# A decoder trunk's odd attention: placement of the sample queries, and the iterations in which sample results are read

## The reference, cut to what matters

```python
# NSA: compressed, selected and window branch, gated;  DSA: an indexer picks the keys
p_c = masked_softmax(s_c, dist_c >= 0);   o_c = p_c @ vc          # compressed keys
p_s = masked_softmax(s_s, mask_s);        o_s = p_s @ sel_v       # selected blocks
p_w = masked_softmax(s_w, mask_w);        o_w = p_w @ kw_v        # window of 256
o_n = gates[..., 0:1] * o_c + gates[..., 1:2] * o_s + gates[..., 2:3] * o_w
isc = relu(qi @ kidx) @ wi;               i_idx = top_k(isc, topk)
o_d = masked_softmax(qd @ kd[i_idx] - m_d * dist) @ vd[i_idx]
return concat([o_n, o_d]) @ w_out
```

## Time and profile before

| | us |
|---|---|
| median of 3 runs | 1462.45 |
| lowest, highest | 1459.09, 1464.04 |
| the profiled execution, its own time | 1457.2 |
| its span in the trace | 1455.3 |
| PE busy | 1395.8 (96%) |
| DVE, ACT, POOL busy | 750.5, 505.5, 398.9 |

### The profile page before, as it was taken

The page is one execution under the profiler, slowest core; times in us unless marked ns, Lnnn a source line. Parts: engine busy times, 40 slices in busy tenths (PEclk is TensorE's granted clock), DMA queues, the critical chain, the costliest instruction groups (busy, mean ns, idle before and its releaser), DMA issues. The chain is left out here.

```text
span 1455.3 us, 27589 instructions
## 1 busy us (share of the span) xinstructions
PE 1395.8 (96%) x11335; PEld 1308.3 (90%) x11335; DVE 750.5 (52%) x1374; ACT 505.5 (35%) x1004; POOL 398.9 (27%) x471
## 2 busy tenths in 40 slices
PE   6999998999999999999899989998999999999996
PEld 5999974899999999999899856776999999999996
DVE  3424777577334343344879755443584343343435
ACT  3321224355213133133532445675454033130311
POOL 3014423464101010016734471022662010010102
PEclk9999999999999999999999989998999999999998
DMA  4343170031313223121522253202223223131301
GB/s 153 118 115 116 30 233 6 3 116 59 117 59 117 72 103 113 62 66 44 118 51 44 59 175 111 59 1 60 87 88 117 68 107 109 66 116 59 117 30 59
DMA packets 87196, 123.86 MB, mean 85 GB/s; under 512 B 24438, under 2 KB 42302, under 8 KB 87040
## 3 DMA queue, kind: packets, MB, share of 16 engines
q1 hardware_dynamic: 82048, 107.00, 23.0%
q0 software_dynamic: 5024, 15.10, 3.5%
HBM read 115.62 MB, written 8.57 MB: 85 GB/s over the span
## 5 line engine op out<-in xcount | busy, mean ns | idle before, releaser
L1025 PE MATMUL ps<-xh,ring_lo 128*128 128x260 f32 (+2 forms) x2496 | 504.3, 283 | 1.4 <-ACT big L1590 1.4
L1025 PEld LDWEIGHTS ps<-xh,ring_lo 128*128 128x128 f32 (+2 forms) x2496 | 383.2, 187 | 3.3 <-ACT big L1590 2.3
L1025 PE MATMUL ps<-xl,wr 128*128 128x260 f32 x1568 | 351.4, 283 | 6.2 <-DVE xl L2060 3.9
L1025 PE MATMUL ps<-xh,wr 128*128 128x260 f32 x1568 | 353.5, 284 | 2.5 <-POOL xl L822 1.2
L1025 PEld LDWEIGHTS ps<-xl,wr 128*128 128x128 f32 x1568 | 255.2, 188 | 8.2 <-DVE xl L2060 5.1
L1025 PEld LDWEIGHTS ps<-xh,wr 128*128 128x128 f32 x1568 | 256.2, 188 | 5.0 <-ACT att L1627 1.4
L840 POOL TENSOR_TENSOR att<-att 128x520 f32<-128x520 f32 (+1 forms) x80 | 77.3, 967 | 548.6 <-DVE att L1986 521.5
L1962 DVE TENSOR_TENSOR ring_lo<-ring,wr 128x1024 fp32r<-128x1024 f32 (+1 forms) x144 | 191.9, 1336 | 62.2 <-ACT wr L1590 62.0
L1025 PE MATMUL ps<-hh,wr 128*128 128x260 f32 x1024 | 222.1, 283 | 0.0
L1025 PE MATMUL ps<-hh,ring_lo 128*128 128x260 f32 x1024 | 221.8, 283 | 0.0
L1025 PE MATMUL ps<-hl,wr 128*128 128x260 f32 x1024 | 221.7, 283 | 0.0
(11 more groups left out here) (353 smaller groups left out, 1679.0 us busy)
## 6 DMA issues: line engine op xcount, KB each, us to landing
ring<-in_w_up SPq DMA_DIRECT2D x16, 2048.0 KB, 7.9
ring<-in_w_down SPq DMA_DIRECT2D x16, 2048.0 KB, 8.0
ring<-in_w_in_e SPq DMA_DIRECT2D x9, 1024.0 KB, 5.4
ring<-in_w_in_e SPq DMA_DIRECT2D x2, 2048.0 KB, 8.5
ring<-in_w_out_e SPq DMA_DIRECT2D x2, 2048.0 KB, 9.1
ring<-in_w_in_o SPq DMA_DIRECT2D x16, 256.0 KB, 5.0
ring<-in_cache_kv POOLq DMA_DIRECT2D x32, 128.0 KB, 2.4
ring<-in_w_out_o SPq DMA_DIRECT2D x8, 512.0 KB, 7.8
```

What stands on the lines that cost most here:

```text
L1025: last = pe.matmul(bank(g, half)[0:width(g), 0:H2], w[:, k, :], x[:, k, cols(half)], start=first, stop=final)
```

## The change

The placing of QI moves from one burst in iteration 9 to iterations 6 (the clearing) and 7 to 10 (one copy each). The placing of QB["n"] moves from iteration 10 to iterations 13 (the clearing) and 14 to 21 (one scaling each). The two copies of new values move from iteration 11 to 22. PE waits for `qb_ok` at 2 in its first sample step, and for 3 in step 7 (iteration 26), where QB["n"] is first used. The last results of the sample branches are read in iterations 53 (s), 71 (d) and 91 (w), and the copies into the mixer's output follow one iteration later: two in 72 for d, two in 92 for w. ACT's `y_hi` waits for `pb_ev` at 5, `y_hi_half` for 7.

```diff
@@ PE, sample_step @@
                 if k == 0:
                     pe.wait_ge(gat[4], 16 * NT)
-                    pe.wait_ge(sm["qb_ok"], 3)
+                    pe.wait_ge(sm["qb_ok"], 2)
...
                 if k == 7:
                     pe.wait_ge(sm["cmpt_ev"], 1)
                     pe.wait_ge(sm["ixs_ev"], 1)
+                    pe.wait_ge(sm["qb_ok"], 3)
@@ ACT @@
             def y_hi_half(half):
 
                 act.wait_ge(sm["q_g"], end_no["sums", len(jobs) - 2 + half] + 1)
+                act.wait_ge(sm["pb_ev"], 7)
...
-                    y_hi(NP + t - TOKENS_D, "pb_ev", 7)
+                    y_hi(NP + t - TOKENS_D, "pb_ev", 5)
@@ DVE @@
+            def place_query(br, g, p):
+
+                r = slice(HD * g, HD * g + HD)
+                h = NP * g + p
+                return dve.tensor_scalar(QB[br][r, h:h + 72 * 7 + 1:72], big[r, L[f"q{br}{p}"], S:T], SLOPE[h], None, ALU.mult)
...
             def sample_queries(t):
-                if t == 9:
+                if t == 6:
                     link(dve.memset(QI, 0.0))
-                    for e in range(4):
-                        r = slice(32 * e, 32 * e + 32)
-                        last = dve.tensor_copy(QI[0:32, e:e + 36 * 7 + 1:36], big[r, L["qi"], S:T])
-                    last.then_inc(sm["qb_ok"], 1)
-                if t == 10:
-                    place_queries("n")
-                if t == 11:
+                if 7 <= t < 11:
+                    e = t - 7
+                    last = dve.tensor_copy(QI[0:32, e:e + 36 * 7 + 1:36], big[32 * e:32 * e + 32, L["qi"], S:T])
+                    if e == 3:
+                        last.then_inc(sm["qb_ok"], 1)
+                if t == 13:
+                    clear_queries("n")
+                if 14 <= t < 14 + NH:
+                    last = place_query("n", *divmod(t - 14, NP))
+                    if t == 13 + NH:
+                        last.then_inc(sm["qb_ok"], 1)
+                if t == 14 + NH:
                     dve.tensor_copy(vals[:, 32:40], big[:, L["vs"], S:T])
                     link(dve.tensor_copy(vals[:, 40:48], big[:, L["vw"], S:T]))
...
+            def sample_result(t):
+
                 for x, (br, (base, n0, *_)) in enumerate(STEP.items()):
-                    if k == base + 9:
+                    at = START + EVERY * (base + 10) + (3 if br == "w" else 1)
+                    acc = ps[7][:, 192:256]
+                    if t == at:
                         dve.wait_ge(sm["pvs_mm"], x + 1)
-                        acc = ps[7][:, 192:256]
                         dve.wait_ge(sm["pt_ev"], x + 1)
...
                             link(dve.tensor_tensor(oN, oN, rsN, ALU.add))
-                            for n, o in enumerate((oN, oD)):
-                                for g in range(2):
-                                    r = slice(HD * g, HD * g + HD)
-                                    dve.tensor_copy(ymix[r, NP * n:NP * n + NP, S:T],
-                                                    o[r, :].rearrange("x (b g p) -> x g p b", g=2, p=NP)[:, g]
-                                                    ).then_inc(sm["pb_ev"], 1)
-
+                    if br != "s" and t == at + 1:
+                        n = 1 if br == "d" else 0
+                        if br == "d":
+                            dve.wait_ge(sm["pb_ev"], 3)
+                        for g in range(2):
+                            r = slice(HD * g, HD * g + HD)
+                            dve.tensor_copy(ymix[r, NP * n:NP * n + NP, S:T],
+                                            (oN, oD)[n][r, :].rearrange("x (b g p) -> x g p b", g=2, p=NP)[:, g]
+                                            ).then_inc(sm["pb_ev"], 1)
...
                     sample_late((t - START) // EVERY - 1)
+                sample_result(t)
```

More of the change, by code:

```diff
@@ L2434, in place_compressed, with clear_queries, place_queries_d @@
                 last.then_inc(sm["kc_ok"], 1)
-            def place_queries(br):
+            def clear_queries(br):
                 link(dve.memset(QB[br], 0.0))
+            def place_query(br, g, p):
+                r = slice(HD * g, HD * g + HD)
+                h = NP * g + p
+                return dve.tensor_scalar(QB[br][r, h:h + 72 * 7 + 1:72], big[r, L[f"q{br}{p}"], S:T], SLOPE[h], None, ALU.mult)
+            def place_queries_d():
+                clear_queries("d")
                 for g in range(2):
-                    r = slice(HD * g, HD * g + HD)
                     for p in range(NP):
-                        h = NP * g + p
-                        last = dve.tensor_scalar(QB[br][r, h:h + 72 * 7 + 1:72], big[r, L[f"q{br}{p}"], S:T],
-                                                 SLOPE[h], None, ALU.mult)
+                        last = place_query("d", g, p)
                 last.then_inc(sm["qb_ok"], 1)
             def sample_queries(t):
-                if t == 9:
+                if t == 6:
                     link(dve.memset(QI, 0.0))
-                    for e in range(4):
-                        r = slice(32 * e, 32 * e + 32)
-                        last = dve.tensor_copy(QI[0:32, e:e + 36 * 7 + 1:36], big[r, L["qi"], S:T])
-                    last.then_inc(sm["qb_ok"], 1)
-                if t == 10:
-                    place_queries("n")
-                if t == 11:
+                if 7 <= t < 11:
[10 more added lines that the diff above has]
+                if t == 14 + NH:
                     dve.tensor_copy(vals[:, 32:40], big[:, L["vs"], S:T])
@@ L2491, in _ @@
                     dve.wait_ge(sm["free_b"], G_IN1 + Z["qd3"] + 1)
-                    place_queries("d")
+                    place_queries_d()
                 if idx == Z["kc"] + 1:
```

## The result

| | before | change |
|---|---|---|
| first comparison, median of 4 runs each | 1461.89 us | 1444.93 us |
| ratio, 95% interval | | 0.9887 (0.9861 to 0.9914) |
| profiled execution: own time, span | 1457.2, 1455.3 us | 1445.01, 1443.2 us |

Two further comparisons of the change gave ratios of 0.9908 (0.9877 to 0.9939) and 0.9867 (0.9842 to 0.9892). Over all executions of this study the kernel before has a mean of 1460.6 us (86 executions, 1451.7 to 1464.8) and the change one of 1445.9 us (15, 1442.2 to 1450.9): 14.7 us less, with a 95% interval of about 1.7 us to either side, from the scatter of both. The three sets of the change have means of 1445.3, 1447.7 and 1444.2 us.

What follows compares the result with a forecast made beforehand. PE, busy 96% of the span, was taken as the bound, leaving its stalls and low clock to win. Stall A 5.7, Stall B 4.5 and s -0.3 gave 9.9 us: 1462.45 to 1452.5 us, 8-in-10 range 1448 to 1459.

Steps and rivals of the forecast that it cites:

- Stall A: PE idle 4.62 us until 846.30, waiting for DVE's unit 11 behind bursts slowed by POOL's products; forecast gain 5.7 us.
- The 0.6 us put on the path ahead of unit 9: Clearing and copies of iterations 7 and 8 now precede unit 9, for which PE already waits: 0.6 us lost.
- A granted clock near 1.0 behind both places: Sign expected in the changed trace behind both stalls, where the granted clock had been 0.54 and 0.60.
- held again: Rival: gather issues or products of about 0.7 us hold each of eight scalings; gain 7.1, 1455.3 us, chance 0.15.
- its rule: DVE two-port copies and scalings and GpSimd exclude each other for a whole instruction, descriptor writing included; placing would be held.
- Stall B: PE idle 3.29 us until 996.70, since DVE waited for window branch values before unit 89's addition; forecast gain 4.5 us.
- The clock term: Gain from PE's clock not falling between 996.7 and 1002.5 us: 1.6 us taken, bounds 0 and 2.3.
- s: Sample branch result now read in iteration 53, behind a multiplication: 0.3 us later, bounds 0 and 0.7.
- The rival that ended slower: Copies, clearing and scalings, 13 held 1.58 us each on PE's path, 20.5 us against 9.9 won: 1473, chance 0.04.
- Clock not recovered: Rival: remaining waits hold PE's clock down and the next waits take part; gain 6.6, 1455.9 us, chance 0.17.
- one stall refilled: Rival: PE waits for ACT in place of the 3.3 us stall, only the 4.62 us one won; 1457 to 1459, chance 0.09.

Runs made afterwards that it cites:

- filler_a: Kernel before with 18 unread matmuls where PE stands still for 4.6 us ahead of unit 12's scores; units 12 to 16 took 6.57 us (8.08 before).
- The filler: Kernel before with 13 unread matmuls where PE stands still for 3.3 us at iteration 89; units 89 to the projection took 16.48 us (19.71 before).
- the second profile: Kernel before run again unedited and profiled a second time: ratio 0.9993, span 1461.0 us where the first profile had 1455.3.
- the tuned one: Changed kernel with placing bursts in iterations 3 and 5, s read in 52, compressed softmax's last part behind unit 9, ACT's DSA splits in 82 to 85; ratio 0.9865.

## Why the prediction was too small

**Stall A: the mechanism right, the size 5.7 against 6.4.** The wait of 4.62 us went, and the clock behind it was worth 1.8 by filler_a (1.7 taken). The 0.6 us put on the path ahead of unit 9 came out as 0.7 (units 6 to 9 in 6.41 us where 5.72 were needed). These three make the 5.7 of the forecast again. Another 0.6 us was won in units 9 to 12 (11.61 us and now 6.06), and no run separates its cause. The timelines show that the kernel before computes the scores of unit 12 in two pieces around the stall (0.70 us at 840.99, 2.70 at 846.30) and the change in one of 1.50. "A granted clock near 1.0 behind both places" held behind the scores of unit 12 but not ahead of them, where both kernels have 0.50. That the copies in 9 and 10 are hidden, and the scalings in 13 to 21 free, held; and no scaling took over 0.3 us beside an issue (a gather's or a store's), which ends the rival "held again" and its rule as far as issues go.

**Stall B: the mechanism right, the size 4.5 against 6.0; this is the failed term.** The 3.3 us were right, and the two copies of iteration 92 did meet POOL's split, at more than was taken (0.4): 1.44 us of DVE, a wait of 0.78 for PE. The clock term failed. I took 1.6 us with 2.3 as the most, from the stretch 996.7 to 1002.5 alone, and took something off for ACT. The filler, which leaves the stall and takes only the low clock away, shows 3.2 us, beyond my upper bound. The trace of the kernel before has PE at the lower clock a second time, further on, which I did not price:

```profile
1008.00:1010.00 2.00, 2.00 (x17) 1.67 (x18) 0.00 (x0) 0.11 (x1) 0.33 (x1) 0.54 0.00 0
1010.00:1012.00 2.00, 2.00 (x16) 1.35 (x17) 1.45 (x3) 1.44 (x3) 0.00 (x0) 0.60 0.00 0
```

ACT's idle time in the earlier trace rows, 12.0 - 8.82 = 3.2 us, was the larger bound and allowed just what came. 3.3 + 3.2 - 0.8 make 5.7 of the 6.0; the last 0.3 us is unexplained.

**s: -0.3 forecast, -0.4 measured.** PE waits 0.34 us on the read.

**From the profile to the median.** By the profiled executions the forecast (1447.3) missed by 2.3 us; by the medians (1452.5 and 1444.9) by 7.6. Of these, 2.1 us are the two terms above (12.0 us of gain and not 9.9). I set off from the median of three runs, 1462.45, which lies 1.9 us above the mean of all executions measured since, and the median of the first comparison, 1444.93, lies 1.0 below the mean of the change: these 2.9 us are luck of the draw. The remaining 2.7 us are what the timed executions won beyond the first profiles. The range was a fault of its own: its lower end allowed a gain of 14.5 us at the most, while one execution of the kernel before differs from the next by up to 13 us.

**Where the 2.7 us are.** The first profiles give 12.0 us, the second 13.6, the timed executions 14.7 (13.0 to 16.4). The granted clock, which is on record for all executions but five, accounts for most of the scatter. The kernel before took 1463.6 us on average in its 26 executions at 0.983, 1456.3 in 8 at 0.987, 1452.5 in 7 at 0.989; the change 1444.2 in 3 at 0.993 and 1449.4 in 4 at 0.988. At the clocks of the two first profiles (0.987 and 0.993) the difference is 12.1 us, as in the stretches. So the rest of the gain is that most executions of the kernel before run at a lower clock than its first profile did (mean 0.984), while the change's mean (0.991) is nearer to its own. Some of that lies behind stall A, where the second profile takes 0.7 us more for units 12 to 16. How much of it the change takes away in a typical execution, no run here shows. Part of the scatter has nothing to do with the change: the start of unit 0 moves between 816.5 and 824.9 us over all profiles, in code that no edit touches.

The rival that ended slower, 13 operations on PE's path at 1.58 us each, is excluded: the longest of them was 0.65 us. "Clock not recovered" is excluded at B by the 1.00 from 984.5 to 996.5 us and at A by the 1.00 from 842 us on, and "one stall refilled" by PE's list, where no wait for ACT is over 0.8 us.

## What to carry to other kernels

A burst of tiny VectorE copies costs little by itself (0.7 and 0.8 us here); beside a run of GpSimd products each costs up to the length of a product, so first move the burst ahead of or behind them, and only then think of spreading it. In a hand-written pipeline a read of an old result belongs behind the unit that the next engine waits for; one place in the order was worth 6 us, three iterations were not needed. When a stall goes, price the lower clock behind it with a filler of unread matmuls in the old kernel, and compare stretches between fixed instructions: they repeat to a tenth of a microsecond where whole times scatter by ten, but only between profiles whose clock fell in the same places. Write down each execution's granted clock beside its time.

## What was not expected of the hardware

PE's granted clock falls to half in some executions where PE has no wait and is busy with small matmuls: from about 826 to 836 us in the kernel before and the change alike (3.2 us in units 0 to 6), and from 983 to 996 in one of three profiles of the change (5.6 us: 23.13 against 18.80 behind unit 88, and 136.24 against 134.94 ahead of it). The same code shows both cases. The kernel with the shortest waits, the tuned one, had the longest profiled execution of its set mainly for this reason.
